# One phase for the norm, filter network and filters of a hybrid encoder block, x loaded from ScalarE's queue, and 64-row transfers for residual and output

## The reference

```python
h = rmsnorm(x, norm_mix_g);  p = h @ w_in                    # 1024 -> 2560
a = rg_lru(conv4(p[:, :512]), forward) + rg_lru(..., backward), times gelu(p[:, 512:1024])
kf = hyena_filters()                                         # depends on parameters alone
b = hyena(conv3(p[:, 1024:]), kf)                            # two long convolutions
x = x + concat(rmsnorm(a), rmsnorm(b)) @ w_out
x = x + hier_moe(rmsnorm(x))                                 # 2 of 32 experts for each token
out = rmsnorm(x, norm_final_g)

def hyena_filters():
    z = sin(ff1 * (feats @ fw1 + fb1))                       # feats: 2048 x 33
    z = sin(ff2 * (z @ fw2 + fb2))
    h = (z @ fw3) * decay                                    # 2048 x (2 directions, 2 orders, 512)
    k = forward and reversed backward half, 4096 taps, over the sum of their magnitudes
    return rfft(k)
```

## Time and profile before

| | |
|---|---|
| median of three runs | 2699.0 us |
| profiled execution | 2701.3 us, its span 2699.5 us |
| granted TensorE clock, mean | 0.910 |
| TensorE busy | 2177.7 us (81%) |
| VectorE, ScalarE, GpSimd busy | 1346.8, 1068.6, 253.0 us |
| moved by DMA | 503.7 MB, 187 GB/s in the mean |

### The profile page before, as it was taken

How to read it: one execution, slowest core, us unless ns; L and a number is a source line. 1 busy time by engine, 2 the same in 40 slices (tenths; PEclk the granted TensorE clock), 3 DMA queues, 4 the chain that set the end, 5 groups by cost and what they waited for, 6 DMA issues and landing times. The chain is left out here.

```text
span 2699.5 us, 30316 instructions
## 1 busy us (share of the span) xinstructions
PE 2177.7 (81%) x8397; PEld 1378.3 (51%) x8398; DVE 1346.8 (50%) x1114; ACT 1068.6 (40%) x1278; POOL 253.0 (9%) x243
## 2 busy tenths in 40 slices
PE   2795999999999697973999479999999999995000
PEld 1452444444444322222778358887878878884000
DVE  5432381835628344544344544648686466554222
ACT  4451321423223132331222155658696566553111
POOL 0361000000000020210000000000000000002110
PEclk8897999999999899986999779999999999997555
DMA  3362223032230498874333176759898678674441
GB/s 138 111 225 82 80 63 109 17 93 80 62 109 10 174 335 330 304 269 154 129 143 131 49 259 225 296 221 392 305 397 310 246 271 305 217 280 163 161 155 65
DMA packets 261720, 503.73 MB, mean 187 GB/s; under 512 B 24481, under 2 KB 103301, under 8 KB 257286
## 3 DMA queue, kind: packets, MB, share of 16 engines
q1 hardware_dynamic: 221414, 408.75, 41.9%
q10 hardware_dynamic: 28448, 51.39, 5.1%
q0 software_dynamic: 11808, 43.00, 4.4%
HBM read 367.79 MB, written 135.27 MB: 186 GB/s over the span
## 5 line engine op out<-in xcount | busy, mean ns | idle before, releaser
L364 PE MATMUL pj<-hT,W 128*128 128x512 f32 x1280 | 556.3, 596 | 10.6 <-DMA fs<-in_fa_signal_dram 10.6
L364 PEld LDWEIGHTS pj<-hT,W 128*128 128x128 f32 x1280 | 244.1, 192 | 313.9 <-issue 313.9
L1545 PE MATMUL p<-wh_hi,x_hi 128*128 128x512 f32 x768 | 309.2, 403 | 11.2 <-DVE wh_lo L1670 11.1
L1670 DVE TENSOR_TENSOR wh_lo<-w_raw,wh_hi 128x2048 fp32r<-128x2048 f32 x128 | 284.7, 2287 | 51.6 <-ACT wh_hi L1634 51.6
L1545 PE MATMUL p<-wh_hi,x_lo 128*128 128x512 f32 x768 | 304.5, 397 | 0.0
L1545 PE MATMUL p<-wh_lo,x_hi 128*128 128x512 f32 x768 | 304.5, 396 | 0.0
L1634 ACT ACTIVATE wh_hi<-w_raw 128x2048 fp32r<-128x2048 f32 x128 | 234.6, 1913 | 0.2
L1545 PEld LDWEIGHTS p<-wh_hi,x_hi 128*128 128x128 f32 x768 | 145.0, 189 | 49.7 <-DVE wh_lo L1670 15.1
L1545 PEld LDWEIGHTS p<-wh_hi,x_lo 128*128 128x128 f32 x768 | 144.9, 189 | 35.0
L1545 PEld LDWEIGHTS p<-wh_lo,x_hi 128*128 128x128 f32 x768 | 145.0, 189 | 32.8
L1545 PE MATMUL pyy<-wy_hi,a_hi 128*128 x392 | 159.7, 407 | 2.3 <-ACT yb L1616 2.3
(11 more groups left out here) (278 smaller groups left out, 3374.2 us busy)
## 6 DMA issues: line engine op xcount, KB each, us to landing
w_raw<-in_exp_w_dram SPq DMA_DIRECT2D x512, 256.0 KB, 4.8
w_raw<-in_exp_w_dram SPq DMA_DIRECT2D x128, 512.0 KB, 8.9
scratch_YB<-yb ACTq DMA_DIRECT2D x50, 512.0 KB
scratch_KA<-kst SPq DMA_DIRECT2D x32, 512.0 KB, 2.7
scratch_YB<-zero SPq DMA_DIRECT2D x4, 4096.0 KB, 14.5
kin<-scratch_KA SPq DMA_DIRECT2D x32, 512.0 KB, 7.0
zin<-scratch_SA SPq DMA_DIRECT2D x32, 512.0 KB, 6.0
scratch_SI<-qo SPq DMA_DIRECT2D x32, 512.0 KB, 3.7
```

The source lines that it names most:

```text
L364: last = pe.matmul(pj[n][:, :], lhs(k), rhs(k, n), start=(k == 0), stop=(k == n_k - 1))
L1545: mm = pe.matmul(acc[:, :], x[:, k, :], w, start=(k == 0 and i == 0), stop=(k == n - 1 and i == 2))
L1670: dve.tensor_tensor(lo, raw[:, j:j + 2, :], hi.bitcast(F32), ALU.subtract).then_inc(lowered, 1)
```

## The change

It makes `load_and_norm` and `filters` one phase, `norm_and_filters`, with one set of buffers (the filters' tiles lie in buffers that the network and the first five tiles of `X` have left):

- ScalarE issues the four loads of x, as its first instructions. SyncE issues the parameters, now with a semaphore for each group: layer 1 waits for three loads, VectorE for eight, layer 2 for two more. The filters' parameters and first decay tiles follow on the same queue.
- The matmuls of the network release VectorE one by one.
- The mean square and root are taken for tiles 0 to 7 and 8 to 15 apart, inside the two range reductions. `X` is normalised in place, tiles 0 to 5 between the two layers, 6 to 15 behind them, so VectorE waits for no copy. ScalarE copies a transposed tile in one instruction. The squares go into PSUM (`junk` is `pa[1]`), and the transposes wait for all 16 squares.
- The filter loop follows without barriers. Its instructions and their waits are as before.

In `output_projection` and `combine` each transfer of xt and of the output becomes two, of 64 rows each, with the semaphore counts doubled.

```diff
+        FIRST = 6
         @block.sync
-            for g in range(GROUPS):
-                sp.dma_start(X[:, g * per:(g + 1) * per, :], x_t[:, g * per:(g + 1) * per, :]).then_inc(x_in[g], 16)
...
         @block.tensor
-            pe.wait_ge(par_in, BASE + 16 * N_PAR)
+            pe.wait_ge(feats_in, 48)
             for n in range(4):
-                last = pe.matmul(flat[n][:, :], w1[:, :], feats[:, n * 512:(n + 1) * 512], start=True, stop=True)
-            last.then_inc(mlp_mm, 1)
+                pe.matmul(flat[n], w1[:, :], feats[:, n * CH:(n + 1) * CH], start=True, stop=True).then_inc(mlp_mm, 1)
...
+            pe.wait_ge(squares, NT)
+            for i in range(NT):
+                pe.wait_ge(xn_ready, i + 1)
+                if i >= 2:
+                    pe.wait_ge(evacuated, i - 1)
...
         @block.scalar
             for g in range(GROUPS):
+                act.dma_start(X[:, g * per:(g + 1) * per, :], x_t[:, g * per:(g + 1) * per, :]).then_inc(x_in[g], 16)
...
+            square(0, NT // 2)
+            root(0)
+            square(NT // 2, NT - per)
+            act.wait_ge(arg_ready, 1)
+            act.activation(z1, arg, ACT.Sin).then_inc(mlp_sin, 1)
+            square(NT - per, NT)
+            turned(0, FIRST)
+            root(1)
+            act.wait_ge(arg_ready, 2)
             act.activation(zzd[0:R, 0, :], arg[0:R, :], ACT.Sin).then_inc(mlp_sin, 1)
             act.activation(zzd[R:P, 1, 1:SEQ][:, ::-1], arg[R:P, 1:SEQ], ACT.Sin).then_inc(mlp_sin, 1)
+            turned(FIRST, NT)
...
         @block.vector
+                for i, part in enumerate((C1, C2, C3)):
+                    step(dve.scalar_tensor_tensor(out=arg, in0=rnd, scalar=-part, in1=arg, op0=ALU.mult, op1=ALU.add))
+                    if i == 0:
+                        mean_square(layer)
...
+            dve.wait_ge(vec_in, 16 * 8)
+            reduce_range(0)
+            dve.wait_ge(gain_in, 16)
+            normalise(0, FIRST)
+            dve.wait_ge(mlp_sin, 1)
+            reduce_range(1)
+            normalise(FIRST, NT)
...
# output_projection
+        def load_x(sp, t, s):
+            for g in range(2):
+                sp.dma_start(xt[HALF * g:HALF * g + HALF, s, :], x_t[ds(t, 1), g].rearrange("a n d -> (a n) d")).then_inc(x_in[s], 16)
-                    sp.dma_start(xt[:, s, :], x_t[s]).then_inc(x_in[s], 16)
+                    load_x(sp, s, s)
...
# combine
-                sp.dma_start(out_t[ds(t, 1)].rearrange("a g n d -> (a g) n d"), out[:, q % 2, :]).then_inc(o_out[q % 2], 16)
+                for g in range(2):
+                    sp.dma_start(out_t[ds(t, 1), g].rearrange("a n d -> (a n) d"), out[HALF * g:HALF * g + HALF, q % 2, :]).then_inc(o_out[q % 2], 16)
```

More of the change, by code:

```diff
@@ L106, in load_and_norm @@
[L106 to L112, removed]
+        ssq, rstd = sb("ssq", [P, NT]), sb("rstd", [P, NT])
@@ L113, in load_and_norm @@
+        kgen, k_ready, abs_ready, summed, fa_done, kst_ready = (sem(n, 0) for n in ("kgen", "k_ready", "abs_ready", "summed", "fa_done", "kst_ready"))
+        norm_mm, norm_ready, k0_ready, inv_ready = (sem(n, 0) for n in ("norm_mm", "norm_ready", "k0_ready", "inv_ready"))
         per = NT // GROUPS
+        FIRST = 6
+        order = [*range(1, N2), 0]
+        tile = lambda j: kt[:, j % 4] if j else kt0
         x_t = dram["x"].rearrange("o (i p) d -> p (o i) d", p=P)
@@ new lines, in _, with store @@
+            sp.dma_start(fa[:, :], dram["fa_filter"]).then_inc(f_in, 16)
+            sp.dma_start(skip[:, :, :], dram["hy_skip"]).then_inc(f_in, 16)
+            def store(i):
+                sp.wait_ge(kst_ready, i + 1)
+                sp.dma_start(dram["KA"][:, :, order[i], :].rearrange("o p c -> p o c"), kst[:, i % 4]).then_inc(kst_out[i % 4], 16)
+            for j in range(N2):
+                if j >= 4:
+                    sp.wait_ge(k_ready, j - 3)
+                sp.dma_start(dec[:, j % 4, :], dram["decay"][:, j, :]).then_inc(dec_in[j % 4], 16)
+                if j >= 6:
+                    store(j - 6)
@@ L133, in _ @@
+            for i in range(N2 - 6, N2):
+                store(i)
+            for s in range(4):
+                sp.wait_ge(kst_out[s], 16 * (N2 // 4))
         @block.gpsimd
@@ L135, in _ @@
             pool.memset(w2[:, :], 0.0).then_inc(w2_zero, 1)
+            pool.wait_ge(w2_zero, 1)
+            pool.memset(ones[:, :], 1.0).then_inc(summed, 1)
+            pool.wait_ge(kgen, 1)
+            pool.wait_ge(summed, 1)
+            pool.memset(acc, 0.0).then_inc(summed, 1)
+            for j in range(N2):
+                pool.wait_ge(abs_ready, j + 1)
+                pool.wait_ge(summed, j + 2)
+                pool.tensor_tensor(acc, acc, ka[j % 2], ALU.add).then_inc(summed, 1)
@@ L148, in _, with square @@
-            act.wait_ge(arg_ready, BASE + 2)
+                act.dma_start(X[:, g * per:(g + 1) * per, :], x_t[:, g * per:(g + 1) * per, :]).then_inc(x_in[g], 16)
+            def square(first, last):
+                for i in range(first, last):
+                    if i % per == 0:
+                        act.wait_ge(x_in[i // per], 16)
+                    if i:
+                        act.wait_ge(squares, i)
+                    act.activation(junk, X[:, i, :], ACT.Square, accum_out=ssq[:, i:i + 1]).then_inc(squares, 1)
@@ new lines, in root, with turned @@
+            def root(n):
+                act.wait_ge(ms_ready, n + 1)
+                half = slice(n * NT // 2, (n + 1) * NT // 2)
+                act.activation(rstd[:, half], rstd[:, half], ACT.Sqrt).then_inc(rstd_ready, 1)
+            def turned(first, last):
+                for i in range(first, last):
+                    act.wait_ge(tp_ready, i + 1)
+                    act.activation(hT[:, :, i * P:(i + 1) * P], pa[i % 2].rearrange("p a (k t) -> p (a k) t", k=4), ACT.Copy).then_inc(evacuated, 1)
@@ L162, in _ @@
+            magnitude(0)
+            magnitude(1)
+            for j in range(2, N2):
+                magnitude(j)
+                evacuate(j - 2)
+            evacuate(N2 - 2)
+            evacuate(N2 - 1)
         @block.vector
@@ L179, in _ @@
             dve.memset(zzd[R:P, 1, 0:1], 0.0)
[L180 to L198, removed]
```

309 lines of the change are left out of this document (129 added, 180 removed).

## The result

The changed kernel takes 2529.4 us (median of 4 runs, 2526.95 to 2530.17) beside 2698.7 us (4 runs, 2696.38 to 2700.37) on the same chip: a ratio of 0.937, 95% interval 0.9355 to 0.9388, or 169 us less. The profiled execution has a span of 2527.2 us against 2699.5, 172.3 less. A second measurement of the same kernel gave 2527.8 us, 0.9363 [0.935, 0.9375].

A forecast was written before the change was run, and what follows sets the result against it. The prediction took `combine` to be bound by output stores on two DMA engines. Its terms 124 + 10 + 37 = 171 us, taken from the median 2699.0, gave 2528 us, with a range of 2508 to 2572.

The forecast's parts named there:

- The bound: In `combine`, output stores in the `[2, 64, 1024]` view run on two DMA engines, busy from start to end.
- The 64-row stores, 124 us: In `combine`, stores spread over all engines, tiles come 5.3 us apart, and 124 us are saved; bounds 95 and 136.
- L: In `combine`, a store's landing time after its issues, taken as 5 us; two tiles take 5.5 + L.
- The transfers' bound, 5.5 us a tile at 384 GB/s: In `combine`, two gathers, a load and a store are 2.1 MB a tile; for the phase 89 us.
- The 64-row residual loads, 10 us: At the start of `output_projection`, SyncE's queue is freed and `gain_ffn` comes earlier: 10 us saved; bounds 3 and 12.
- One phase, 37 us: In the first phases, the first filter matmul begins at 66, 36.4 us earlier: 37 us saved; bounds 20 and 41.
- the term for the small loads: In the first phase, layer 1's three loads were taken to let it start at 8.0 us, with x's loads beside them.
- the buffers bind: Rival in `combine`: the two output buffers set the pace with landing 8.5 us, 7.0 a tile, 2557 us; chance 0.2.
- The small loads are held by x: Rival in the first phase: parameters wait behind x on the same engines, 17 us lost, 2545 us; chance 0.16.
- No spread: Rival for stores and residual loads: a 64-row transfer still uses two engines, only 37 us remain, 2662 us; chance 0.03.
- one engine: Rival for 64-row transfers: each half is served by one and the same engine, slower at 2835 us; chance 0.02.
- Everything at its best: Rival for the whole kernel: transfers alone bound `combine`, 2510 us; chance 0.09.

The follow-up runs named there:

- experiments 1: The kernel before the change with only the 64-row stores of `combine` added: 2575.9 us, 0.9538 of the kernel before.
- 4: The changed kernel with each 64-row store given a view of 4 by 16 rows, output rows permuted within a tile: 2583.1 us, 0.9567.
- 5: The changed kernel with each 64-row store given a view of 8 by 8 rows, output rows permuted within a tile: 2549.4 us in a single run.
- 6: The changed kernel with each tile's output stored as one 128-row transfer, output rows in another order: 2524.6 us, 0.9355.
- Experiment 8: The changed kernel with x's four loads issued from SyncE's queue behind the network's parameters, none from ScalarE's: 2531.2 us, 0.9377.
- 9: The changed kernel with ScalarE taking the sine of layer 1 before it squares tiles 8 to 11: 2530.1 us, 0.9371.
- 11: The changed kernel with four output buffers, layer 1's sine before squares 8 to 11, and four of eight `vec` loads issued by GpSimd: 2519.6 us, 0.9331.

## Why the prediction was right

The predicted time was 2528 and the measured one 2529.4. The sum's 171 us stand beside 169.3 and 171.7 for the medians and 172.3 for the spans. The mechanism of each part is what the runs show; that the sum came out within 2 us owes something to luck, since errors of 2 to 5 us in its terms cancel. By its steps:

- *The bound* was read rightly. The `[2, 64, 1024]` view ran on two engines; experiments 1, 4, 5 and 6 show it by taking the stores alone and by making the count 4, 8 and 16.
- *The 64-row stores, 124 us*: 122.8 in the changed kernel, 123.9 alone. Tiles 0 to 11 were 5.74 apart and not 5.3 (4.8 us more in all), the last four 4.0 and not 4.5, issue and landing of the end 4.2 and not 5.9 (3.7 us less). They nearly cancel: 83.4 us from the first scale's end to the last landing, against 82.2. The term that was too small is L. The forecast had 5 us from a tile's two issues to its landing, and it was 6.2. The other 5.5 us of the loop were right: with L = 6.2 a tile takes (5.5 + 6.2) / 2 = 5.8 us, and from tile 1 to tile 11 it took 59.2 / 10 = 5.9. With four buffers it is 5.1.
- *The transfers' bound, 5.5 us a tile at 384 GB/s*, was not one: 410 GB/s was reached, 5.1 us.
- *The 64-row residual loads, 10 us*: 11.9 in the changed kernel, 11.6 alone, some 11 over all traces. The wait for `gain_ffn` fell away; tile 1's pA came 9.0 us sooner behind `wo` than before (8.8 predicted). The slow matmuls of tile 1 were worth 16.40 - 13.94 = 2.5 us and not 1.5, so that tile 2's came 11.45 us sooner.
- *One phase, 37 us*: 35.45 in the changed kernel, 33.6 in the mean of all traces. The steps were each late: layer 1 at 10.09 (8.0), arguments at their end 20.8 (16.0), sine's end 36.7 (30.7), second sines' end 58.7 (53.3), first filter matmul 68.57 (66). The weakest step is the term for the small loads, which were forecast at 8.0 "with x's loads beside them" for the matmul's three and at nothing for VectorE's eight: these took 7.7 us from issue to landing, and the last one released VectorE at 17.81. The first matmuls' lateness gives 2.1 of the arguments' 4.8 us and `vec` the other 2.7. The second group of x, forecast at 16.5, was there at 18.90, but VectorE didn't wait for its squares. The third, at 28.76, delayed ScalarE's squares 8 to 11, and the sine began 2.9 us behind its argument. Experiment 8 took away x beside the small loads, 9 the squares ahead of the sine, and 11 half of `vec`'s queue besides; none brought the filters forward. The end of the phase repaid half: from the second sines' end to the filters are 9.8 us and not 12.7. The ten copies came at 1.14 us a tile, inside the forecast 1.1 to 1.25, TensorE and ScalarE taking turns. But the filters need no copy, only TensorE, which is through with the transposes before ScalarE has copied the last pair:

```profile
66.75 1.98 PE L191 MATMUL fp<-ident,X 128*128 128x128 f32 x16 [0.30 <-ACT hT L257]
67.85 1.94 ACT L257 ACTIVATE hT<-fp 128x1024 f32<-128x1024 f32 x2 [0.33 <-PE fp L191]
```

- *Not foreseen*: the 2.5 us of `experts`. 1.9 of it is a shorter wait ahead of GpSimd's first gather, and why it is shorter is open.

Of the rivals, "the buffers bind" at 7.0 a tile fell with a landing of 6.2 and not 8.5, but in small it is true: two buffers cost 7 to 9 us. "The small loads are held by x" is true in direction, 5 us in place of 17. "No spread" and "one engine" are excluded by the windows and by experiments 4 and 5. "Everything at its best", 2510, wasn't reached; four buffers and a part of `vec` on another queue came nearest, at 2519.6.

## What to carry to other kernels

Before a stage is made faster, take the DMA share of a stretch where one kind of transfer runs alone, times 16: if it is about 2, look at the outermost dimension of the view, not at the engines that wait. A split pays where it raises that dimension (123 us here) and seems to cost a little where it doesn't (0.3 us for each 512 KB tile here, the rows' distance changed with it). And a share near 1 is no proof that transfers bind: one more buffer, or the same data with fewer transfers, tells.

## What the runs showed of the hardware

- A store through a view whose outer dimension is m: tail shares 0.12 (m = 2), 0.22 (m = 4) and 0.46 (m = 8), which times 16 are 1.9, 3.5 and 7.4 engines, at 49, 79 and 140 GB/s, so 25, 22 and 19 GB/s for each engine that is used.
- Behind a load of xt in the `[2, 64, 1024]` view, the issues of the next loads on the same queue took 6.92 and 11.22 us, and 0.59 and 1.06 us behind two loads of 64 rows.
- Loads of 0.2 KB on SyncE's queue landed in 2.3 us with x behind them on the same queue, and in 7.7 us with x's 2 MB loads on ScalarE's queue at the same time. The Trainium skill, page "DMA: Bandwidth & Descriptors", section "Queues, rings and completion order", has an engine take a packet of several descriptors from one ring before it turns to the next, which would delay small loads beside large ones. No run here shows single turns.
- TensorE's granted clock behind 8.03 us of idle time and two short matmuls was 0.50, the lower of its two levels, for 3.3 us, then 0.65 in the mean of 3 us, then 1.00. Without the idle time it was 1.00 throughout, and the same tile's matmuls took 13.94 us and not 16.40.
- In long stretches of `combine` a DMA share of 0.99 went with 364 GB/s, 1.01 with 388 and 1.02 with 410.
- GpSimd's first gather of `experts` came 1.9 us sooner behind its index copy with the joined phase far ahead of it (0.94 us of idle time in ten traces, 1.22 in one, against 2.78 to 2.85 in three without it). The cause was not tried.
